# Merge turns by sevens in all four groups, a second seven in dilated pair 1, and two of four weight sums by accumulating DMAs

## The chip, the cores and the metric

The kernel runs on one core of a Trainium2 chip. Its time is the device time in microseconds (us) of one execution, the median of three runs. PE is the matmul engine (TensorE), DVE the vector engine (VectorE), ACT the scalar engine (ScalarE), POOL is GpSimd, SP is SyncE. The rows come from one profiled execution.

## The reference

One decoder layer on x of 256 tokens by 2048 columns, float32: a SwiGLU feed-forward (d_ff 5632), then two token mixers side by side (8 heads of dilated sliding-window attention with partial rotary, 8 heads of forgetting attention), merged by sigmoid gates, a second SwiGLU, a final RMSNorm.

```python
x = x + 0.5 * swiglu(rmsnorm(x, ffn1_norm), w_gate1, w_up1, w_down1)
proj = rmsnorm(x, mix_norm) @ w_in      # q_d k_d v_d q_f k_f v_f f_logit g_d g_f
merged = (sigmoid(g_d + b_gate_dil) * (y_dil @ w_proj_dil)
          + sigmoid(g_f + b_gate_fox) * (y_fox @ w_proj_fox))
x = x + merged @ w_out
x = x + 0.5 * swiglu(rmsnorm(x, ffn2_norm), w_gate2, w_up2, w_down2)
return rmsnorm(x, final_norm)
```

## The kernel before

Every float32 product is made of three matmuls in a reduced format: each operand is split into a rounded part (hi) and a rest (lo), and hi x hi, hi x lo and lo x hi are summed in PSUM. The weights come from HBM in loads of 1024 KB (`raw`, 4 buffers, `raw[:, l % LOADS]`), each holding 4 tiles of 128 rows by 512 columns. Two tiles are one *slab*. ACT rounds a slab into `w_hi`, DVE subtracts to get `w_lo`, PE multiplies. In the mixer part a ring of 4 slots (`MIX_RING`) holds the slabs: ACT rounds slab n + 4 when PE has done slab n (`slab_done`), DVE splits it when `hi_ready` says so, and PE waits for `lo_ready`. Each engine executes its own instructions in the order written.

Two weight matrices of the same width (called gate and up) times the two token tiles are four block products. Done directly, a group of 4 weight tiles of each is 4 slabs of 12 matmuls, 48 in all. *By seven* (Strassen-like), the group is 7 slabs of 6 matmuls, 42 in all, in exchange for sums. The token sums (`pair_sums`, `merge_pairs`, ...) are made once. The weight sums T3, T1, T2, T4 are made by DVE for every group (`dil_sum`, `merge_sum`), each over 128x1024 elements, into two buffers (T3 and T2 share one, T1 and T4 the other).

The parts in order: a first FFN (10 steps of 33 slabs), six *dilated pairs* (`dil_pair`; c = 0 to 5, of `D_SLABS` slabs, q/k, q/k, v for either mixer; with attention woven in), the first merge part (24 direct slabs of gate logits and projections, `MERGE_FIRST`), three *merge steps* (`merge(q)`, q = 0 to 2), a last down product and the second FFN. Of the pairs, c = 2 has two sevens and the others one.

A merge step of before has 41 slabs (`MERGE_STEP`): sevens at slabs 0, 9 and 18, the two direct gate slabs of group 3 at 7 and 8, its two direct up slabs at 16 and 17, 8 projection slabs from 25 (`M_PROJ_AT`), 8 down slabs from 33. DVE's order in it: at slab o it splits slab o + 4, with the sums of that slab's seven ahead of it; at o = 21 to 26 it combines the products into gate and up; after every second down slab it adds two banks into `xres` (`add_down`, L1872).

SP issues all weight loads in order, each behind a wait that the buffer's earlier slabs are split (`D_FREE`, `M_FREE`: the load l waits for that many slabs of the step). POOL issues in the FFNs the accumulating DMAs of the down products (`xres` += `gate_buf`, 512 KB, L1734), and nothing in the mixer part.

Of the kernel before, what the change touches and what calls it, by code (L numbers as in the profile page):

```python
# [19 lines left out]
F32 = mybir.dt.float32  # L20
# [45 lines left out]
D_SLABS, D_LOADS = (19, 19, 22, 19, 19, 19), 8  # L66
# [9 lines left out]
D_FREE = (_QK_FREE, _QK_FREE, _V_FREE, _QK_FREE, _QK_FREE, _QK_FREE)  # L76

D_SUMS, D_COMBINED = (0, 4, 8, 16, 20, 24), 5
# [4 lines left out]
M_PAIR_AT, M_PAIR_GROUPS, M_PAIR_LOADS = (0, 9, 18), (0, 1, 2), ((0, 1), (3, 4), (6, 7))  # L83
M_DIRECT_AT, M_DIRECT_GROUP, M_DIRECT_LOADS = (7, 16), 3, (2, 5)
# [3 lines left out]
M_PAIRS, M_SUMS, M_COMBINED = 3, 12, 5  # L88

M_THIRD, M_SPLIT_COUNT = 2, (1, 3, 2)  # L90
# [23 lines left out]
SUM_PLACE = {T3: 0, T2: 0, T1: 1, T4: 1}  # L114
SUMS_STEP = 4 * PAIRS
# [17 lines left out]
def merge_slab(r):  # L133

    for pair, first in enumerate(M_PAIR_AT):
        if first <= r < first + PAIR_SLABS:
            return "paired", pair, r - first
    for d, first in enumerate(M_DIRECT_AT):
        if first <= r < first + 2:
            return "direct", d, r - first  # L140
    return "rest", None, r - M_PROJ_AT
# [103 lines left out]
def build(nc, x, ffn1_norm, ffn1_w_gate, ffn1_w_up, ffn1_w_down, mix_norm, w_in, b_forget,  # L245
# [83 lines left out]
    tab_at = nc.sbuf_base  # L329
# [30 lines left out]
    gains = sb("gains", [P, 3 * KT])  # L360
    gain_rows = nc.alloc_sbuf_tensor_at("gain_rows", [KT, P], F32, offset=bias_at)
    squares = sb("squares", [P, TT, NN])
    end_sum = sb("end_sum", [P, TT])
    mean = sb("mean", [P, TT])
    root = sb("root", [P, TT])
    rstd = sb("rstd", [P, TT])
    rstd_q = sb("rstd_q", [P, TT])
    newton = sb("newton", [P, TT])
    neg_max = sb("neg_max", [P, TT])
    denom = sb("denom", [P, TT])  # L370
    inv_denom = sb("inv_denom", [P, TT])
# [4 lines left out]
    M1, M6, M7, M5, GATE, UP1, UP0 = 0, 1, 2, 3, 4, 6, 7  # L376
    DOWN_BANKS = (0, 2, 6, 4)
# [31 lines left out]
    def dil_sums_at(c, which):  # L409

        if c < F_PAIR:
            return dil_sums[:, SUM_PLACE[which]]
        return v_sb[:, SUM_PLACE[which], D_MIX:2 * D_MIX].rearrange("p (a b) -> p a b", b=CH)

    def dil_source(e):

        c, r, (kind, which, o) = dil_slab(e)
        if kind == "paired":
            what, part = PRODUCTS[o]
            if what == "sum":  # L420
                return dil_sums_at(c, part), None
            l = D_SEVEN[c][which][2][what == "gate"]
            return raw[:, l % LOADS, part::2, :], l
# [4 lines left out]
    def third_sums(x):  # L428


        return x[:, :, :].rearrange("p (g a b) c -> p g a b c", a=2, b=2)[:, 0:3, :, 0, P:2 * P]

    def merge_source(r):

        kind, which, o = merge_slab(r)
        if kind == "paired":
            what, part = PRODUCTS[o]
            if what == "sum":
                return merge_sums[SUM_PLACE[part]], None
            l = M_PAIR_LOADS[which][what == "gate"]  # L440
            return raw[:, l % LOADS, part::2, :], l
        l = M_DIRECT_LOADS[which] if kind == "direct" else M_PROJ_LOADS + o // 2
# [23 lines left out]
    dil_summed = sem("dil_summed")  # L466
    dil_m1_copied = sem("dil_m1_copied")
# [5 lines left out]
    merge_summed = sem("merge_summed")  # L473
    merge_m1_copied = sem("merge_m1_copied")
# [92 lines left out]
    DIL_TURNS = ((), (0, 1, 3, 4), (0, 1, 4, 6), (), (), ())  # L567
# [27 lines left out]
    with block:  # L595

        @block.sync
        def _(sp):
# [92 lines left out]
            for q in range(MERGES):  # L691
# [60 lines left out]
        def _(pe):  # L752
# [111 lines left out]
            def down(place, offset, count, base, next_too=False):  # L864
# [3 lines left out]
                for n in range(NN):  # L868
# [3 lines left out]
                    banks = down_banks(n)  # L872
# [155 lines left out]
            def dil_pair(c):  # L1028
# [26 lines left out]
                def seven_slab(s, group, o):  # L1055
                    bank, lhs = ((D_M7, of_sums(group, S3)), (D_M1, of_tile(group, 0, 0)),
                                 (D_M5, of_sums(group, S1)), (D_M6, of_sums(group, S2)),
                                 (D_UP0, of_sums(group, S4)), (D_GATES + 1, of_tile(group, 1, 1)),
                                 (D_GATES, of_tile(group, 1, 0)))[o]
# [178 lines left out]
            for g, banks in enumerate((A, C)):  # L1238
# [8 lines left out]
            def merge(q):  # L1247
# [3 lines left out]
                def of_pair(p, s):  # L1251
                    if p != M_THIRD:
                        return lambda j: (merge_hi[:, p, s, j], merge_lo[:, p, s, j])
                    if s == S4:
                        return lambda j: (fourth_hi[:, j], fourth_lo[:, j])
                    return lambda j: of_x(CT * s + 2 * j, 1)
# [1220 lines left out]
```

## Time and profile before

| | before |
|---|---|
| median of 3 runs | 2041.95 us (2041.85 to 2042.55) |
| span of the profiled execution | 2040.2 us |
| PE, DVE, ACT, POOL busy | 99%, 91%, 62%, 4% |
| weight loads (SP's queue) | 401.64 MB, 56.1% of 16 DMA engines |
| accumulating DMAs (POOL's queue) | 38.28 MB, 11.3% |

The profiled execution's own time is its span of 2040.2 us and what lies around it; the median of the runs is 1.75 us above the span. Busy times of matmuls overlap by pipelining, so the granted clock and the starts of matmuls say more than busy time.

### The profile page before, as it was taken

The numbers are of one execution on the slowest core, as the hardware profiler recorded it, in microseconds if no ns is written. First come the engines' busy times: TensorE is split into PE (matmuls) and PEld (weight loads), VectorE is DVE, ScalarE is ACT, GpSimd is POOL, SyncE is SP. The second block draws the span as 40 slices with busy tenths as digits, with TensorE's granted clock in tenths as the row PEclk, the third lists the DMA queues.
The fourth block names the chain that finished last, engine by engine and source line by source line (L and its number), as shares of the span: only waits on it lengthen the run. The fifth ranks groups of instructions, "written<-read, shape, count | busy, mean of one in ns | idle before, by whom it ended". The sixth has DMA issues, their size and how long they took to land.

```text
span 2040.2 us, 26364 instructions
## 1 busy us (share of the span) xinstructions
PE 2027.8 (99%) x9204; PEld 1678.7 (82%) x9204; DVE 1858.9 (91%) x1897; ACT 1267.5 (62%) x1474; POOL 87.6 (4%) x80
## 2 busy tenths in 40 slices
PE   9999999999999999999999999999999999999998
PEld 7888888888888888888888888888888888888886
DVE  7999999999999798887689999799999999999997
ACT  7666666666666556666556556466666666666664
POOL 0000000000000000000000000000000000000000
PEclk9999999999999999999999999999999999999999
DMA  8578777787877455554536575655878777877773
GB/s 301 206 211 259 230 236 246 227 236 227 246 247 235 157 186 183 198 177 157 183 134 227 189 243 182 211 186 192 242 223 250 244 232 211 260 225 240 247 231 127
DMA packets 222143, 441.03 MB, mean 216 GB/s; under 512 B 7648, under 2 KB 7824, under 8 KB 221936
## 3 DMA queue, kind: packets, MB, share of 16 engines
q1 hardware_dynamic: 202112, 401.64, 56.1%
q0 software_dynamic: 19744, 38.28, 11.3%
q8 instruction: 47, 0.77, 0.1%
q14 instruction: 32, 0.26, 0.0%
q10 hardware_dynamic: 208, 0.08, 0.0%
HBM read 400.13 MB, written 2.10 MB: 197 GB/s over the span
## 4 chain that ended last, share of the span: by engine, by line
PE 98%; DVE 1%; ACT 0%; DMA 0%; issue 0%; SPq 0%; ACTq 0%; DVEq 0%
PE ps L765 16%; PE ps L767 16%; PE ps L766 16%; PE ps L778 12%; PE ps L780 12%; PE ps L779 12%; PE ps L1002 2%; PE ps L1003 2%; PE ps L1001 2%; PE ps L1050 2%; PE ps L1052 2%; PE ps L1051 2%; PE ps L856 1%; PE ps L834 0%; DMA xres<-in_x 0%; PE ps L1169 0%
## 5 line engine op out<-in xcount | busy, mean ns | idle before, releaser
L1788 DVE TENSOR_TENSOR w_lo<-raw,w_hi 128x1024 fp32r<-128x1024 f32 x280 | 337.9, 1219 | 7.2 <-ACT w_hi L1356 4.9
L1356 ACT ACTIVATE w_hi<-raw 128x1024 fp32r<-128x1024 f32 x280 | 290.8, 1053 | 72.6 <-PE ps L767 54.0
L1356 ACT ACTIVATE w_hi<-sums 128x1024 fp32r<-128x1024 f32 x160 | 169.8, 1063 | 204.8 <-PE ps L767 71.4
L1788 DVE TENSOR_TENSOR w_lo<-sums,w_hi 128x1024 fp32r<-128x1024 f32 x160 | 195.3, 1222 | 33.8 <-ACT w_hi L1356 31.1
L765 PE MATMUL ps<-w_hi,hT_hi 128*128 128x512 f32 x536 | 208.8, 390 | 0.0
L767 PE MATMUL ps<-w_hi,hT_lo 128*128 128x512 f32 x536 | 208.5, 389 | 0.0
L766 PE MATMUL ps<-w_lo,hT_hi 128*128 128x512 f32 x536 | 208.5, 389 | 0.0
L1788 DVE TENSOR_TENSOR more_lo<-raw,more_hi 128x1024 fp32r<-128x1024 f32 x140 | 169.2, 1219 | 6.6 <-ACT more_hi L1356 5.6
L765 PE MATMUL ps<-w_hi,xT_hi 128*128 128x512 f32 x424 | 170.1, 401 | 0.0
L1356 ACT ACTIVATE more_hi<-raw 128x1024 fp32r<-128x1024 f32 x140 | 146.4, 1054 | 32.6 <-PE ps L767 23.8
L767 PE MATMUL ps<-w_hi,xT_lo 128*128 128x512 f32 x424 | 165.7, 391 | 0.0
L766 PE MATMUL ps<-w_lo,xT_hi 128*128 128x512 f32 x424 | 165.2, 390 | 0.0
L1734 POOL DMA_DIRECT2D xres<-gate_buf x72 | 84.9, 1179 | 1848.3 <-ACT gate_buf L1490 1803.3
L1356 ACT ACTIVATE more_hi<-sums 128x1024 fp32r<-128x1024 f32 x80 | 85.1, 1063 | 99.1 <-DVE sums L1770 24.1
L778 PE MATMUL ps<-w_hi,xT_hi 128*128 128x512 f32 x354 | 139.8, 395 | 0.0
L780 PE MATMUL ps<-w_hi,xT_lo 128*128 128x512 f32 x354 | 138.1, 390 | 0.0
L779 PE MATMUL ps<-w_lo,xT_hi 128*128 128x512 f32 x354 | 137.9, 390 | 0.0
L1675 ACT ACTIVATE w_hi<-raw 128x1024 fp32r<-128x1024 f32 x87 | 92.2, 1060 | 63.6 <-PE ps L767 51.8
L2128 DVE TENSOR_TENSOR w_lo<-raw,w_hi 128x1024 fp32r<-128x1024 f32 x85 | 102.2, 1220 | 20.2 <-ACT w_hi L1576 20.2
L1576 ACT ACTIVATE w_hi<-raw 128x1024 fp32r<-128x1024 f32 x85 | 89.1, 1057 | 47.2 <-PE ps L1052 31.0
L2317 DVE TENSOR_TENSOR w_lo<-raw,w_hi 128x1024 fp32r<-128x1024 f32 x87 | 104.8, 1220 | 14.9 <-ACT w_hi L1675 14.9
L767 PEld LDWEIGHTS ps<-w_hi,hT_lo 128*128 128x128 f32 x536 | 100.6, 188 | 20.9
(366 smaller groups left out, 5007.4 us busy)
## 6 DMA issues: line engine op xcount, KB each, us to landing
raw<-in_ffn_w_up SPq DMA_DIRECT2D x88, 1024.0 KB, 5.5
raw<-in_ffn_w_down SPq DMA_DIRECT2D x88, 1024.0 KB, 5.3
raw<-in_ffn_w_gate SPq DMA_DIRECT2D x87, 1024.0 KB, 5.4
raw<-in_w_in SPq DMA_DIRECT2D x80, 1024.0 KB, 5.0
xres<-gate_buf POOLq DMA_DIRECT2D x72, 512.0 KB, 5.5
raw<-in_w_out SPq DMA_DIRECT2D x16, 1024.0 KB, 5.1
raw<-in_w_proj_dil SPq DMA_DIRECT2D x8, 1024.0 KB, 5.5
raw<-in_w_proj_fox SPq DMA_DIRECT2D x8, 1024.0 KB, 5.2
```

Source lines behind the costliest of these rows:

```text
L765: nc.tensor.matmul(acc, hi, hi_w[:, j], start=first and j == 0, stop=False)
L766: nc.tensor.matmul(acc, hi, lo_w[:, j], start=False, stop=False)
L767: done = nc.tensor.matmul(acc, lo, hi_w[:, j], start=False, stop=last and j == 1)
L778: nc.tensor.matmul(acc, hi, hi_w[:, j], start=first and j == 0, stop=False)
L779: nc.tensor.matmul(acc, hi, lo_w[:, j], start=False, stop=False)
L780: done = nc.tensor.matmul(acc, lo, hi_w[:, j], start=False, stop=last and j == 1)
L1356: nc.scalar.activation(slot_hi(place, offset), src, ACT.Copy).then_inc(hi_ready, 1)
L1576: nc.scalar.activation(slot_hi(place, r), src, ACT.Copy).then_inc(hi_ready, 1)
L1675: nc.scalar.activation(slot_hi(place, offset), src, ACT.Copy).then_inc(hi_ready, 1)
L1788: nc.vector.tensor_tensor(slot_lo(place, offset), step_source(r)[0], slot_hi(place, offset).bitcast(F32), ALU.subtract).then_inc(lo_ready, 1)
L2128: nc.vector.tensor_tensor(slot_lo(place, r), dil_source(e)[0], slot_hi(place, r).bitcast(F32), ALU.subtract).then_inc(lo_ready, 1)
L2317: nc.vector.tensor_tensor(slot_lo(place, offset), merge_source(offset)[0], slot_hi(place, offset).bitcast(F32), ALU.subtract).then_inc(lo_ ...
```

## The change

In the merge steps all four groups are done by seven, at slabs 0, 7, 14 and 21; the direct slabs go. A step has 44 slabs. Dilated pair 1 takes the layout of pair 2, with a second seven (22 slabs). In all sevens of the mixer part the order of the products changes: gate 1, T3, T2, gate 0, up 1, T1, T4. DVE makes T3 and T2 only. T1 is made by a DMA from POOL that adds gate tiles into the up tiles of the raw buffer, T4 by one that adds T2 into the gate tiles. So T1 and T4 are read from the raw buffers, and these are freed by slabs 5 and 6 of the seven. Signs move into the token sums and into `rstd_n`. The combining adds of a merge step go from slabs 21 to 26 to slabs 25 to 28, with one add more (UP0 has its own bank), and the banks are numbered anew (`M_M1` ...; `merge_banks` swaps the down banks of all steps but the last). The token sums of the fourth group are made at slab 13 of the first merge part. Tables are laid out anew in SBUF. The FFNs are left as they are.

```diff
-D_SLABS, D_LOADS = (19, 19, 22, 19, 19, 19), 8
+D_SLABS, D_LOADS = (19, 22, 22, 19, 19, 19), 8
...
-D_SEVEN, D_GATE, D_UP = zip(_QK, _QK, _V, _QK, _QK, _QK)
-
-_QK_FREE, _V_FREE = (-6, -4, -2, 0, 2, 4, 6, 11), (-6, -4, -2, 0, 2, 7, 9, 11)
...
+D_SEVEN, D_GATE, D_UP = zip(_QK, _V, _V, _QK, _QK, _QK)
+
+_QK_FREE, _V_FREE = (-6, -4, -2, 0, 2, 4, 6, 12), (-6, -4, -2, 0, 2, 8, 9, 11)
...
-M_PROJ_AT, M_PROJ_LOADS, M_DOWN_AT, MERGE_STEP, MERGE_LOADS = 25, 8, 33, 41, 16
-
-M_FREE = (-6, -4, -2, 0, 5, 7, 9, 14, 16, 18, 23, 25, 27, 29, 31, 33)
...
+M_PAIR_AT, M_PAIR_GROUPS, M_PAIR_LOADS = (0, 7, 14, 21), (0, 1, 2, 3), ((0, 1), (2, 3), (4, 5), (6, 7))
+M_PROJ_AT, M_PROJ_LOADS, M_DOWN_AT, MERGE_STEP, MERGE_LOADS = 28, 8, 36, 44, 16
+
+M_FREE = (-6, -4, -2, 0, 6, 7, 13, 14, 20, 21, 27, 28, 30, 32, 34, 36)
...
+M_PRODUCTS = (("gate", 1), ("sum", T3), ("sum", T2), ("gate", 0), ("up", 1), ("sum", T1), ("sum", T4))
...
                 for o in seven(0):
-                    if o == 1:
+                    if q > 0 and o == 1:
+                        pe.wait_ge(gated, used + 2 * TT)
+                    if o == 2:
                         pe.wait_ge(gated, used + TT)
-                    if o == 5:
+                        pe.wait_ge(added, base)
+                    if q == 0 and o == 4:
                         pe.wait_ge(gated, used + 2 * TT)
-                        pe.wait_ge(added, base)
...
+                    part = M_PRODUCTS[o][1]
+                    if part == T1:
+                        act.wait_ge(merge_t1_added[pair], (q + 1) * 16)
+                    elif part == T4:
+                        act.wait_ge(merge_t4_added[pair], (q + 1) * 16)
...
+            def merge_add(q, p):
+
+                place, (up_l, gate_l) = merge_place(q), M_PAIR_LOADS[p]
+                up, gate = raw[:, up_l % LOADS], raw[:, gate_l % LOADS]
+                pool.wait_ge(merge_summed, q * M_SUMS + 2 * p + 1)
+                pool.wait_ge(raw_landed[gate_l % LOADS], place.landed(gate_l))
+                pool.dma_start(up[:, 0::2, :], gate[:, 0::2, :], accum_op=ALU.add)\
+                    .then_inc(merge_t1_added[p], 16)
+                pool.wait_ge(merge_summed, q * M_SUMS + 2 * p + 2)
+                pool.wait_ge(lo_ready, place.slab(M_PAIR_AT[p] + 1))
+                pool.dma_start(gate[:, 1::2, :], merge_sums[1], accum_op=ALU.add)\
+                    .then_inc(merge_t4_added[p], 16)
...
                 if which == T3:
-                    dve.wait_ge(lo_ready, place.slab(at - 2))
+                    if pair > 0:
+                        dve.wait_ge(lo_ready, place.slab(M_PAIR_AT[pair - 1] + 2))
                     dve.wait_ge(raw_landed[up_l % LOADS], place.landed(up_l))
-                    made = nc.vector.tensor_tensor(out, up[:, 1::2, :], up[:, 0::2, :], ALU.subtract)
...
+                    made = nc.vector.tensor_tensor(merge_sums[0], up[:, 1::2, :], up[:, 0::2, :], ALU.add)
+                else:
+                    if pair > 0:
+                        dve.wait_ge(merge_t4_added[pair - 1], (q + 1) * 16)
+                        dve.wait_ge(lo_ready, place.slab(M_PAIR_AT[pair - 1] + 3))
+                    elif q > 0:
+                        dve.wait_ge(merge_t4_added[M_PAIRS - 1], q * 16)
                     dve.wait_ge(raw_landed[gate_l % LOADS], place.landed(gate_l))
...
+                if kind == "paired" and o == 0:
+                    merge_sum(q, pair, T2)
+                if kind == "paired" and o == 5 and pair + 1 < M_PAIRS:
+                    merge_sum(q, pair + 1, T3)
+                if offset == MERGE_STEP - 2 and q + 1 < MERGES:
                     merge_sum(q + 1, 0, T3)
...
-                    if o == 21:
+                    if o == 25:
                         dve.wait_ge(merge_m1_copied, q + 1)
-                        dve.wait_ge(slab_done, place.slab(22))
-                        nc.vector.tensor_tensor(u2, ps[:, M6], partial[:, PART_M1],
+                        dve.wait_ge(slab_done, place.slab(25))
+                        nc.vector.tensor_tensor(u2, ps[:, M_M6], partial[:, PART_M1],
                                                 ALU.add).then_inc(merge_combined, 1)
```

The dilated pairs get the same: `dil_add` on POOL with the waits of `merge_add`, T2 ahead of the seven's first slab, T3 one slab before the seven.

## Rows read from the trace of the kernel before

**Rows 1.** The page: busy time, then slices of PE, its clock, and DMA.
```profile
PE 2027.8 (99%) x9204; PEld 1678.7 (82%) x9204; DVE 1858.9 (91%) x1897; ACT 1267.5 (62%) x1474; POOL 87.6 (4%) x80
...
PEclk9999999999999999999999999999999999999999
```

**Rows 2.** The page: the chain that ended last, by engine.
```profile
PE 98%; DVE 1%; ACT 0%; DMA 0%; issue 0%; SPq 0%; ACTq 0%; DVEq 0%
```

**Rows 3.** Windows over merge steps 0 and 1: window, busy us, clock, DMA share, GB/s.
```profile
1064.10:1149.50 85.40, 84.74 (x375) 69.28 (x374) 80.86 (x79) 46.55 (x48) 0.00 (x0) 1.00 0.61 205
1149.50:1233.60 84.10, 84.10 (x375) 69.40 (x375) 78.36 (x75) 46.86 (x48) 0.00 (x0) 1.00 0.62 207
```

**Rows 4.** Timeline of PE (start, us, what): slab 0 of steps 0, 1, 2; slab 1.
```profile
1064.13 0.39 PE L778 MATMUL ps<-w_hi,merge_hi 128*128 128x512 f32 x1
...
1149.54 0.39 PE L778 MATMUL ps<-w_hi,merge_hi 128*128 128x512 f32 x1
...
1150.90 0.39 PE L778 MATMUL ps<-w_hi,xT_hi 128*128 128x512 f32 x1
...
1233.62 0.39 PE L778 MATMUL ps<-w_hi,merge_hi 128*128 128x512 f32 x1
```

**Rows 5.** Timeline of ACT around the start of step 1.
```profile
1141.64 1.06 ACT L1675 ACTIVATE w_hi<-merge_sum 128x1024 fp32r<-128x1024 f32 x1 [1.66 <-PE ps L767]
1144.36 1.06 ACT L1675 ACTIVATE w_hi<-raw 128x1024 fp32r<-128x1024 f32 x1 [1.66 <-PE ps L767]
...
1149.80 1.06 ACT L1675 ACTIVATE w_hi<-merge_sum 128x1024 fp32r<-128x1024 f32 x1 [1.66 <-PE ps L767]
1151.16 1.06 ACT L1675 ACTIVATE w_hi<-raw 128x1024 fp32r<-128x1024 f32 x1 [0.30 <-PE ps L780]
```

**Rows 6.** Timeline of DVE around the start of step 1.
```profile
1142.73 1.23 DVE L2317 TENSOR_TENSOR w_lo<-merge_sum,w_hi 128x1024 fp32r<-128x1024 f32 x1 [0.36 <-ACT w_hi L1675]
...
1151.26 1.22 DVE L2317 TENSOR_TENSOR w_lo<-merge_sum,w_hi 128x1024 fp32r<-128x1024 f32 x1
1152.39 1.22 DVE L1872 SCALAR_TENSOR_TENSOR xres<-ps,xres 128x1024 f32<-128x1024 f32 x1
1153.53 1.22 DVE L2317 TENSOR_TENSOR w_lo<-raw,w_hi 128x1024 fp32r<-128x1024 f32 x1
```

**Rows 7.** Instructions of line 1734, the accumulating DMAs: ns min/median/max, then landing.
```profile
L1734 POOL DMA_DIRECT2D xres<-gate_buf x72: 1168/1179/1222, 104.4 to 1949.6; - x72
...
DMA to landing us min/median/max: 5.2/5.5/9.0
```

**Rows 8.** The four of one FFN step, issued at 228.62, 234.15, 239.50, 244.93: landing.
```profile
DMA to landing us min/median/max: 8.9/8.9/8.9
...
DMA to landing us min/median/max: 7.3/7.3/7.3
...
DMA to landing us min/median/max: 5.3/5.3/5.3
...
DMA to landing us min/median/max: 5.6/5.6/5.6
```

**Rows 9.** Windows: us, POOL busy, clock, DMA share, GB/s; accumulate alone, then loads.
```profile
241.00:244.00 3.00, 0.00 (x0) 1.00 1.05 171
...
1138.00:1140.00 2.00, 0.00 (x0) 1.00 1.02 396
1158.00:1161.00 3.00, 0.00 (x0) 1.00 1.04 403
```

**Rows 10.** Groups of DVE from 1040 to 1059, ahead of step 0: token sums.
```profile
L2326 DVE TENSOR_TENSOR merge_x<-xT_hi,xT_lo 128x1024 f32<-128x1024 f32 x1 | 1.2, 1217 | 0.0
L2346 DVE TENSOR_TENSOR merge_lo<-merge_pairs,merge_hi 128x1024 fp32r<-128x1024 f32 x1 | 1.2, 1216 | 0.0
...
L2330 DVE TENSOR_TENSOR merge_third<-merge_x 128x256 f32<-128x256 f32 x1 | 0.4, 424 | 0.0
```

**Rows 11.** SP's loads from 1136 to 1190: issue to landing.
```profile
DMA to landing us min/median/max: 4.8/5.0/5.8
```

More of the change, by code:

```diff
@@ L418, in dil_source @@
         if kind == "paired":
-            what, part = PRODUCTS[o]
+            what, part = D_PRODUCTS[o]
+            up_l, gate_l = D_SEVEN[c][which][2]
+            if what == "sum" and part in (T3, T2):
+                return dil_sums_at(c, part), None
             if what == "sum":
-                return dil_sums_at(c, part), None
-            l = D_SEVEN[c][which][2][what == "gate"]
+                return raw[:, (up_l if part == T1 else gate_l) % LOADS, (part == T4)::2, :], None
+            l = gate_l if what == "gate" else up_l
             return raw[:, l % LOADS, part::2, :], l
@@ L436, in merge_source @@
         if kind == "paired":
-            what, part = PRODUCTS[o]
+            what, part = M_PRODUCTS[o]
+            up_l, gate_l = M_PAIR_LOADS[which]
+            if what == "sum" and part in (T3, T2):
+                return merge_sums[part == T2], None
             if what == "sum":
-                return merge_sums[SUM_PLACE[part]], None
-            l = M_PAIR_LOADS[which][what == "gate"]
+                return raw[:, (up_l if part == T1 else gate_l) % LOADS, (part == T4)::2, :], None
+            l = gate_l if what == "gate" else up_l
             return raw[:, l % LOADS, part::2, :], l
-        l = M_DIRECT_LOADS[which] if kind == "direct" else M_PROJ_LOADS + o // 2
+        l = M_PROJ_LOADS + o // 2
         return raw[:, l % LOADS, o % 2 * 2:o % 2 * 2 + 2, :], l
@@ L1237, in _ @@
                     e += 1
-            for g, banks in enumerate((A, C)):
+            for g, banks in enumerate((A, T)):
                 pe.wait_ge(gate_pre, (g + 1) * TT)
@@ L1570, in round_dil @@
                 src, l = dil_source(e)
-                if l is None:
-                    act.wait_ge(dil_summed, D_SUMS[c] + 4 * which + PRODUCTS[o][1] + 1)
+                part, seven = D_PRODUCTS[o][1] if kind == "paired" else None, D_BEFORE[c] + which
+                if l is None and part in (T1, T4):
+                    added_by = dil_t1_added if part == T1 else dil_t4_added
+                    act.wait_ge(added_by[seven % 2], (seven // 2 + 1) * 16)
+                elif l is None:
+                    act.wait_ge(dil_summed, 2 * seven + (part == T2) + 1)
                 else:
@@ L2200, in _ @@
                 if r == last + 6:
+                    dve.wait_ge(slab_done, place.slab(last + 6))
                     dve.wait_ge(dil_combined, merged + 2)
```

312 lines of the change are left out of this document (152 added, 160 removed).

## The prediction

> **What bounds the kernel now.** I read the page first. PE is busy for 99% of the span at a granted clock of full speed, and DVE for 91% [rows 1]. The chain that ended last is PE for 98% [rows 2]. So a PE instruction less is a gain, and every wait that PE gets is a loss: there is no slack in which to hide one. Next I read the stretch that the change rebuilds. One merge step of before takes 84.1 us with PE busy for 84.10 of 84.10 us, DVE for 78.4 us; the first of the three takes 85.4 us with PE busy for 84.74 [rows 3]. The starts of slab 0 say the same: 1064.13, 1149.54 and 1233.62, so 85.41 and 84.08 us [rows 4]. The first step therefore holds 1.3 us of stall and the second none.
>
> Then the pace of the engines inside the step. Two slabs of one product begin at 1149.54 and 1150.90: 1.36 us for 6 matmuls [rows 4]. ScalarE, which rounds slab n + 4 when slab n is done, starts every 2.72 us in the direct part and every 1.36 us in the turns by seven [rows 5]. A VectorE operation over 128x1024 takes 1.22 us, but the next starts 1.13 to 1.14 us after it (1151.26, 1152.39, 1153.53) [rows 6]; I use 1.135. So a seven costs PE 7 x 1.36 = 9.5 us, and VectorE in before 7 splits and 4 sums, 11 x 1.135 = 12.5 us. VectorE is the slower one in every seven. What saves before is the pair of direct slabs between the sevens: 9 slabs are 15.0 us of PE and 13 x 1.135 = 14.8 us of VectorE.
>
> **The change, part by part.** (1) *Matmuls.* A group done directly is 48 matmuls, by seven 42. One group per merge step and one in dilated pair 1 change: 4 x 6 x 0.227 = 5.4 us less on PE, of it 1.36 us per merge step.
>
> (2) *VectorE.* Per seven, T1 and T4 go to accumulating DMAs, so 7 splits and 2 sums stay: 9 x 1.135 = 10.2 us, still above PE's 9.5 us. But the four sevens of a merge step now follow each other over 28 slabs, 38.1 us of PE, with no direct slab between. The lead that PE has is small: the weight ring has 4 slots, and a split is through 0.26 us (ScalarE's start) + 1.09 (rounding) + 1.22 = 2.6 us after its slot came free, while PE needs it 3 x 1.36 = 4.1 us after. That is 1.5 us of slack.
>
> (3) *The accumulating DMAs.* T4 is the one to follow. POOL issues it after T2 is summed and slab 0 of the seven is split, because it adds into the bytes that slab 0 reads. Queued behind it: ScalarE waits for it before it rounds slab 6 of the same seven, and its in-order queue holds slab 7 behind that. VectorE waits before the split of slab 6, and behind that stands T2 of the next seven, which overwrites the operand that the DMA reads. Then comes slab 0 of the next seven, which releases the next T4. It is a closed loop. With L from issue to landing, one turn of it is 0.1 (semaphore, estimated) + L + 1.09 (rounding, 1141.64 to 1142.73) + 1.135 (split of slab 6) + 1.135 (T2) + 1.22 (split of slab 0) = L + 4.7 us [rows 5, 6]. It costs nothing only if L is below 9.5 - 4.7 = 4.8 us. The same kind of DMA, 512 KB in SBUF accumulated by POOL, took 5.2 us at least, 5.5 in the median and 9.0 at most, of which 1.18 us is POOL's issue [rows 7]. So no L in the trace fits.
>
> Which L? The four of one FFN step landed after 8.9, 7.3, 5.3 and 5.6 us [rows 8]. The short ones had the DMA engines to themselves at first, the long ones had loads beside them. Alone, an accumulate moves 171 GB/s with the engines full (241 to 244); loads move 396 to 403 GB/s [rows 9]. A seven of the new merge step needs two loads of 1.05 MB, 2 x 2.6 us, and two accumulates of 0.52 MB, 2 x 3.1 us: 11.4 us of full engines per seven of 9.5 us of PE. The weight loads are freed by splits 5 and 6 of a seven (the new list of free slots), so they start 2 to 3 us before T4 every time. L is then a contended one. I take 7.3, the row with a load in flight for part of the time; 5.3 and 8.9 are the ends.
>
> (4) *The sum of a merge step*, zero at PE's start of slab 0. Split 3 starts at 0.26 + 1.09 = 1.35. Then follow the residual add, split 4, T3, splits 5 and 6, T2 and split 7, seven pitches on: split 7 starts at 9.3 and is done at 10.5. T4 of the second seven: split 13 starts at 10.5 + 0.1 + L + 1.09 = 11.7 + L. Split 14 is done at 15.2 + L, split 21 one loop later at 19.9 + 2L, split 27 at 22.3 + 3L, and PE ends slab 27 at 23.7 + 3L. Without waits it would be 38.1, so the loss is 3L - 14.4. T4 of the first seven is covered by four direct slabs. One more wait comes behind it: slab 28 writes the banks of M1 and M6, and the add that reads them (now at slab 25, before at 21 with the projections at 25) stands behind splits 28 and 29: 3.4 us after split 27 starts plus 0.7, against PE's 1.22 + 1.36, so 1.5 us. The wait for the residual add, moved from product 5 to product 2 of the first seven, costs 3.7 - 2.7 = 1.0 us there, but the wait at slab 13 swallows it (PE would ask at 18.7, the split is done at 20.2). Per step: 3L - 14.4 + 1.5 - 1.36 = 3L - 14.3, which is +7.6 us at 7.3. At L = 5.3 VectorE's own 10.2 us per seven is the slower: split 21 done at 10.5 + 2 x 10.2 = 30.9, split 27 at 30.9 + 0.1 + 5.3 + 1.09 + 1.22 = 38.6, PE's end 40.0, so +2.0. At 8.9 it is +12.4.
>
> (5) *The first merge step* held 1.3 us of stall already, which these waits replace: -1.3. Its fourth group of token sums adds a 1.22 us add, four of 0.42 us and a split of 1.22 us on VectorE, and one copy on ScalarE [rows 10]. They lie beside direct slabs of 2.72 us with 1.135 us of split each; nothing, and up to 1.3 us if that cover is gone, since VectorE has no gap there from 1049.8 on.
>
> (6) *Dilated pairs.* Pair 1 gains 1.36 us. In the other five only sums move, where PE already waits for nothing, so VectorE's relief is worth 0. T4 there has direct slabs beside it. The tightest is the second seven of pairs 1 and 2, whose gate load is freed one split later (8 for 7). Counted from the end of slab 3, that load is issued at about 2.6 and landed at about 8 (loads landed 4.8 to 5.8 us after issue [rows 11]), split 11 is done at 10.4, T4 landed at 17.8, split 17 done at 20.1. PE asks at 5 x 1.36 + 2 x 2.72 + 6 x 1.36 = 20.4. So 0; at L = 8.9 it is 1.3 us in each, 2.6 together. POOL's queue holds nothing else in this part.
>
> Sum: 3 x 7.6 - 1.3 - 1.4 = **+20.1 us**. The profiled execution has a span of 2040.2 us, 1.75 us below the median of 2041.95 us; that remainder is launch and end, and stays. Forecast: 2041.95 + 20.1 = **2062 us**.
>
> **A rule of the Trainium skill.** An accumulate with full engines moved 171 GB/s here [rows 9]. The Trainium skill, page "DMA: Bandwidth & Descriptors", section "Where 436 GB/s comes from", says that for transfers from SBUF to SBUF the fabric side of 435 GB/s binds. By it, as an estimate, an accumulate would need 1.2 us, and the change would come out as in rival A. The trace speaks against it, with its 171 GB/s.
>
> **The rivals.** *A: no loss, VectorE alone sets the pace.* If L is 3.6 us or less (5.3 less the 1.7 us or so by which a transfer at the loads' 400 GB/s is shorter), the loop is 8.3 us and the sevens run at 10.2. Then split 27 is done at 30.9 + 6 x 1.135 = 37.7, PE ends at 39.1, and a step is 1.0 + 1.5 - 1.36 = +1.1: in all 3.3 - 2.7 = +0.6, so 2042.6 us. With L = 5.3 it is 3 x 2.0 - 2.7 = +3.3, 2045 us. For it: the short landings. Against it: each T4 has loads before it. Together 0.10. *B: faster.* If the loop does not bind and the add at slab 25 is in time, PE's 5.4 us and the 1.3 us of the first step come back: 2035 us. It decides at L + 4.7 below 9.5 and needs VectorE below 9.5 us per seven too, and nine pitches are 10.2. 0.03. *C: full engines.* The 11.4 us of DMA per seven put T4 behind both loads each time: L = 8.9, 3 x 12.4 - 2.7 + 2.6 = +37, 2079 us. For it: the engines are asked for more than they give. Against it: as the loop lengthens, the demand falls to 11.4 of 12 us. 0.17. *The forecast*, L from about 6 to 8.3: 0.70.
>
> **How the numbers follow.** The range goes from the short landing (2045) to C (2079). Changes under about 0.2%, 4 us, can't be told from none. Slower is the forecast with C, 0.87; within 0.2% is A, 0.10; faster is B, 0.03.
>
> **What would show it.** In the changed kernel's profile: PE idle of some 20 us or more, nearly all inside the three merge steps, released by splits of slabs 13, 14, 20, 21 and 27 and by the add before slab 28; POOL's accumulates with a landing near 7 us; slab 0 of the steps some 92 us apart; the FFNs unchanged. ScalarE's waits there would name the accumulating DMA. If the landing is below 5.5 us in the merge steps, or the steps are under 86 us, the loop argument is wrong. If the loss lies in the dilated pairs, step 6 is.

## The result and the profile after

The changed kernel takes 2086.43 us (median of 5 runs, 2083.32 to 2087.92), the kernel before 2042.08 us beside it: a ratio of 1.0214, with a 95% interval of 1.0202 to 1.0226. The forecast was 2062 us with a range of 2045 to 2079. The sign was right, the loss more than twice the forecast, and above the range. The profiled execution took 2084.43 us with a span of 2082.6 us.

The page of the changed kernel: busy time, granted clock, the chain that ended last by engine and by line (to set beside [rows 1] and [rows 2]).

```profile
PE 2038.6 (98%) x9180; PEld 1679.2 (81%) x9180; DVE 1848.7 (89%) x1893; ACT 1279.1 (61%) x1486; POOL 134.8 (6%) x120
...
PEclk9999999999999999999999999999999999999999
...
PE 88%; DMA 5%; DVE 4%; ACT 1%; issue 1%; SPq 0%; ACTq 0%; DVEq 0%; POOLq 0%
PE ps L781 15%; PE ps L783 15%; PE ps L782 15%; PE ps L794 10%; PE ps L796 10%; PE ps L795 10%; DMA raw<-merge_sum 4%; PE ps L1019 2%; PE ps L1017 2%; PE ps L1018 2%; DVE w_lo L2357 1%; PE ps L1066 1%; PE ps L1068 1%; PE ps L1067 1%; PE ps 
```

PE has 24 matmuls less and is busy for 10.8 us more, which no count of instructions explains. T4's DMA (raw<-merge_sum), which was not there, stands on the chain for 4% of the span. The windows over the three merge steps, from slab 0 to slab 0 and the last to the first slab after it (columns as in [rows 3]):

```profile
1068.76:1163.87 95.11, 86.86 (x369) 68.81 (x368) 79.96 (x78) 48.86 (x51) 9.84 (x9) 0.98 0.88 242
1163.87:1261.95 98.08, 88.21 (x369) 70.19 (x368) 76.61 (x73) 49.30 (x51) 9.42 (x8) 0.95 0.77 220
1261.95:1361.23 99.28, 89.85 (x378) 72.07 (x376) 75.79 (x73) 50.29 (x53) 7.07 (x6) 0.93 0.70 206
```

In the kernel before they took 85.41, 84.08 and 85.03 us. The last, from 1233.62 to 1318.65, has PE busy throughout:

```profile
1233.60:1318.60 85.00, 85.00 (x383) 70.26 (x382) 76.80 (x74) 47.82 (x50) 0.00 (x0) 1.00 0.60 203
```

So the steps cost +9.7, +14.0 and +14.3 us, and slab 0 of the first starts 4.6 us later (1068.76 for 1064.13 [rows 4]): +42.6 us in all, the whole difference of the spans (42.4). The FFNs and everything behind are unchanged. Two things stand in the columns: PE's idle time (8 to 10 us per step), and a granted clock of 0.95 and 0.93 where it was 1.00, with PE busy for 88 to 90 us on work that took 84.

The chain through step 1 (start, us, what), without its short pieces of idle time:

```profile
1170.90 1.22 DVE w_lo L2357
1172.12 1.14 DVE merge_sum L2338
1173.26 1.15 DVE w_lo L2357
...
1174.93 9.65 DMA raw<-merge_sum
1184.61 1.06 ACT w_hi L1679
...
1186.84 1.22 DVE merge_sum L2338
1188.06 1.15 DVE w_lo L2357
...
1189.79 6.40 DMA raw<-merge_sum
1196.21 1.07 ACT w_hi L1679
...
1198.45 1.22 DVE merge_sum L2338
1199.67 1.14 DVE w_lo L2357
...
1201.55 9.78 DMA raw<-merge_sum
1211.36 1.06 ACT w_hi L1679
...
1212.45 1.24 DVE w_lo L2357
```

This is the closed loop of the prediction's step 3, operation by operation: T4's DMA, the rounding of slab 6, its split (at 1185.70 and 1197.3, which the chain shows as a gap), T2 (L2338), the split of slab 0, the next DMA. From 1174.93 to 1189.79 it takes 14.86 us with a landing of 9.65, from there to 1201.55 11.76 with 6.40, so L + 5.2 and L + 5.4; I had L + 4.7. The rest is POOL's start, 0.6 us after the split of slab 0 is done (1188.06 + 1.15), which I had estimated at 0.1. The landings of T4's DMA over the three steps, and a row each of a matmul behind the last wait of step 1 and of the same kind of matmul later:

```profile
L1754 POOL DMA_DIRECT2D raw<-merge_sum x12: 1179/1179/1200, 1068.0 to 1299.7; - x12
...
DMA to landing us min/median/max: 5.0/7.4/9.8
```

```profile
1213.73 0.80 PE L794 MATMUL ps<-w_hi,xT_hi 128*128 128x512 f32 x1 [4.19 <-DVE w_lo L2357]
1214.32 0.63 PE L795 MATMUL ps<-w_lo,xT_hi 128*128 128x512 f32 x1
1214.75 0.63 PE L796 MATMUL ps<-w_hi,xT_lo 128*128 128x512 f32 x1
...
1222.29 0.39 PE L781 MATMUL ps<-w_hi,yT_hi 128*128 128x512 f32 x1
1222.51 0.39 PE L782 MATMUL ps<-w_lo,yT_hi 128*128 128x512 f32 x1
```

The matmuls after the idle 4.19 us start 0.43 us apart instead of 0.23. The windows say the same (the granted clock is the third figure from the end):

```profile
1213.70:1217.90 4.20, 4.17 (x9) 2.94 (x10) 4.17 (x5) 3.10 (x4) 0.00 (x0) 0.50 0.70 239
1220.00:1224.00 4.00, 4.00 (x19) 3.31 (x18) 3.96 (x6) 1.84 (x2) 0.00 (x0) 1.00 0.83 278
```

So PE was granted half its clock, 1.2 GHz for 2.4, after it had been idle for 4.19 us. It happens again after idle times of 3.97, 4.16 and 3.71 us (at 1186.97, 1285.24 and 1311.58), and in step 0 after 1.99 us:

```profile
1091.83 0.68 PE L794 MATMUL ps<-w_hi,xT_hi 128*128 128x512 f32 x1 [1.99 <-DVE w_lo L2357]
```

The stretches at half clock last 3.5 to 5.7 us. The Trainium skill, page "TensorE: Matmul & The Clock Gate", section "Loop structure matters more than you think", warns of it: a loop in which matmuls wait for DMAs runs them at the lower clock. The trace agrees, and the prediction had no such term.

### The profile page after: what moved, and what is told of

Its sections match the earlier page's. It is cut to its first block, busy times and chain, and to the rows that moved or that the text cites. A ratio compares the mean times of both kernels' runs of the same rounds, so it can differ in the third digit from the quotient of the medians.

```text
span 2082.6 us, 26407 instructions
## 1 busy us (share of the span) xinstructions
PE 2038.6 (98%) x9180; PEld 1679.2 (81%) x9180; DVE 1848.7 (89%) x1893; ACT 1279.1 (61%) x1486; POOL 134.8 (6%) x120
## 4 chain that ended last, share of the span: by engine, by line
PE 88%; DMA 5%; DVE 4%; ACT 1%; issue 1%; SPq 0%; ACTq 0%; DVEq 0%; POOLq 0%
PE ps L781 15%; PE ps L783 15%; PE ps L782 15%; PE ps L794 10%; PE ps L796 10%; PE ps L795 10%; DMA raw<-merge_sum 4%; PE ps L1019 2%; PE ps L1017 2%; PE ps L1018 2%; DVE w_lo L2357 1%; PE ps L1066 1%; PE ps L1068 1%; PE ps L1067 1%; PE ps L872 1%
## 5 line engine op out<-in xcount | busy, mean ns | idle before, releaser
L1832 DVE TENSOR_TENSOR w_lo<-raw,w_hi 128x1024 fp32r<-128x1024 f32 x280 | 337.9, 1219 | 6.9 <-ACT w_hi L1350 4.6
L1350 ACT ACTIVATE w_hi<-raw 128x1024 fp32r<-128x1024 f32 x280 | 290.8, 1053 | 72.4 <-PE ps L783 53.7
L1679 ACT ACTIVATE w_hi<-raw 128x1024 fp32r<-128x1024 f32 x108 | 112.9, 1057 | 131.1 <-PE ps L783 64.8
L794 PE MATMUL ps<-w_hi,xT_hi 128*128 128x512 f32 x384 | 156.8, 408 | 24.8 <-DVE w_lo L2357 23.7
L2357 DVE TENSOR_TENSOR w_lo<-raw,w_hi 128x1024 fp32r<-128x1024 f32 x108 | 130.2, 1220 | 55.3 <-ACT w_hi L1679 55.3
L2170 DVE TENSOR_TENSOR w_lo<-raw,w_hi 128x1024 fp32r<-128x1024 f32 x100 | 121.2, 1222 | 41.2 <-ACT w_hi L1574 38.3
L781 PE MATMUL ps<-w_hi,xT_hi 128*128 128x512 f32 x392 | 157.4, 401 | 0.0
L1574 ACT ACTIVATE w_hi<-raw 128x1024 fp32r<-128x1024 f32 x100 | 104.9, 1057 | 63.5 <-PE ps L1068 25.4
```

Source lines behind the costliest of these rows:

```text
L781: nc.tensor.matmul(acc, hi, hi_w[:, j], start=first and j == 0, stop=False)
L794: nc.tensor.matmul(acc, hi, hi_w[:, j], start=first and j == 0, stop=False)
L1350: nc.scalar.activation(slot_hi(place, offset), src, ACT.Copy).then_inc(hi_ready, 1)
L1574: nc.scalar.activation(slot_hi(place, r), src, ACT.Copy).then_inc(hi_ready, 1)
L1679: nc.scalar.activation(slot_hi(place, offset), src, ACT.Copy).then_inc(hi_ready, 1)
L1832: nc.vector.tensor_tensor(slot_lo(place, offset), step_source(r)[0], slot_hi(place, offset).bitcast(F32), ALU.subtract).then_inc(lo_ready, 1)
```

## The experiments

All runs are set against the kernel before on the same chip (2041.9 to 2042.2 us). The table gives what most of them are read by: where slab 0 of the first merge step starts, the length of the three steps (slab 0 to slab 0), the mean granted clock over the span, and T4's landing in them (minimum, median, maximum). The kernels below the second row differ from it only from the merge steps and their loads on, and yet their slab 0 starts anywhere from 1068.8 to 1072.2: differences in time of 2 to 3 us between single kernels say little, the lengths of the steps say more.

| kernel | us | ratio, 95% interval | slab 0 | steps | clock | T4 landing |
|---|---|---|---|---|---|---|
| before | 2042.1 | | 1064.1 | 85.4, 84.1, 85.0 | 0.999 | |
| after | 2086.4 | 1.0202 to 1.0226 | 1068.8 | 95.1, 98.1, 99.3 | 0.992 | 5.0/7.4/9.8 |
| T1 and T4 by VectorE | 2075.0 | 1.0141 to 1.0175 | 1070.6 | 96.2, 92.1, 93.1 | 0.998 | |
| T1 by VectorE | 2070.9 | 1.0121 to 1.0155 | 1069.7 | 92.8, 92.5, 92.4 | 0.999 | 5.0/6.4/8.2 |
| T4 by VectorE | 2075.0 | 1.0140 to 1.0174 | 1071.4 | 94.4, 91.7, 95.4 | 0.997 | |
| half of T4's bytes | 2073.9 | 1.0138 to 1.0172 | 1070.1 | 92.1, 94.1, 93.2 | 0.998 | 3.3/7.2/8.1 |
| light loads, sevens | 2073.2 | 1.0137 to 1.0171 | 1071.2 | 93.2, 92.6, 93.0 | 0.993 | 5.0/5.0/9.9 |
| light loads, all | 2056.6 | 1.0057 to 1.0087 | 1071.7 | 87.2, 86.8, 87.6 | 0.998 | 5.0/5.0/5.5 |
| loads held back | 2101.7 | 1.0272 to 1.0306 | 1072.2 | 105.4, 101.2, 102.4 | 0.988 | 5.0/5.0/9.1 |
| PE kept busy | 2083.2 | 1.0186 to 1.0220 | 1069.7 | 95.8, 94.9, 99.1 | 0.997 | 5.0/7.1/10.3 |

**Both sums by VectorE.** Without POOL's queue, in place:

```diff
-                pool.dma_start(up[:, 0::2, :], gate[:, 0::2, :], accum_op=ALU.add)\
...
-                pool.dma_start(gate[:, 1::2, :], merge_sums[1], accum_op=ALU.add)\
...
+                    nc.vector.tensor_tensor(raw[:, up_l % LOADS, 0::2, :], raw[:, up_l % LOADS, 0::2, :],
+                                            raw[:, gate_l % LOADS, 0::2, :], ALU.add)\
...
+                    nc.vector.tensor_tensor(raw[:, gate_l % LOADS, 1::2, :], raw[:, gate_l % LOADS, 1::2, :],
+                                            merge_sums[1], ALU.add).then_inc(merge_t4_added[pair], 16)
```

> In the merge steps both T1 and T4 are added by VectorE in place, into the same bytes, instead of by POOL's DMAs; the layout of four sevens stays, the dilated pairs keep their DMAs. Theory (loop through the accumulating DMA): the loop is gone, VectorE's own work sets the pace: 37 pitches of 1.135 us from split 3 to split 27, so PE ends slab 27 at 45.9 us instead of 38.1, a step is about +8 us on before, no wait of PE over 2 us, and the clock stays at full speed: 2071 us. Rival 1 (the accumulates are the whole loss): 2045 to 2050 us. Rival 2 (VectorE was the bound all along in the changed kernel): adding two operations per seven makes it worse than the changed kernel, over 2090 us.

2075.0 us for 2071 expected. T3 (L2321) of two sevens one after the other in the chain of step 1:

```profile
1184.08 1.22 DVE merge_sum L2321
...
1196.57 1.22 DVE merge_sum L2321
```

12.49 us: the 11 operations of 1.135 us of the prediction, against PE's 9.5. Four sevens without direct slabs between them lose some 8 us in steps 1 and 2 (10.8 in step 0) with no DMA at all, because VectorE is slower than PE in each. The accumulating DMAs were meant to take that away, and cost more than it.

**One of the two by VectorE.**

> In the merge steps T1 is added by VectorE in place, T4 stays with the DMA. Loop theory: T4's landing gets shorter because one accumulate per seven less competes (from 8 to 9 us down to 6 to 7), the loop is then near VectorE's ten operations, 11.35 us per seven: +5 to +8 us per step, 2061 to 2072 us. Rival (T4's landing does not depend on the other accumulate): VectorE's extra operation fits in its waits and nothing changes, 2084 to 2088 us.

Inside the range, 2070.9 us. T4's landing fell from 7.4 to 6.4 us in the median although T4 itself is untouched: T1's 512 KB were part of its contention. The loop with 6.4 + 5.2 = 11.6 us and VectorE's 10 operations (11.35 us) are then nearly level.

> In the merge steps T4 is added by VectorE in place, T1 stays with the DMA. Loop theory: T1 is not in the loop, so VectorE's ten operations set the pace: 34 pitches to split 27, PE's slab 27 ends at 42.5, +4.5 us per step, no half clock: 2061 us. Rival (any accumulate in these stretches costs its landing): close to the changed kernel, over 2075 us.

A miss: 2075.0 us for 2061, and at the edge of what the rival said. I had looked at T4's loop alone. Its chain in step 1 shows another one behind it:

```profile
1185.42 10.25 DMA raw<-in_w_in
...
1196.32 10.26 DMA raw<-raw
...
1207.69 2.88 DVE w_lo L2359 x3
```

The gate load of the fourth seven takes 10.25 us where loads took 5.0 in the median [rows 11], T1's DMA may only start when it has landed and takes 10.26, and only then is the slab of T1 rounded. Load and accumulate follow each other, both slow.

**Fewer bytes.** Half of T4's operand is left out:

```diff
-                pool.dma_start(gate[:, 1::2, :], merge_sums[1], accum_op=ALU.add)\
+                pool.dma_start(gate[:, 1:2, :], merge_sums[1][:, 0:1], accum_op=ALU.add)\
```

> The DMA that makes T4 in the merge steps moves only one of its two tiles, 256 KB, so half of T4 is left without its sum; instructions and waits are the same. Loop theory: landing shorter by 1.5 to 2 us, each step by about 3 times that, 4.5 to 6 us, and fewer half-clock stretches: 2066 to 2072 us. Rival (VectorE's pace or the weight loads are the bound): within 3 us of the changed kernel.

2073.9 us, just above its range: half of T4's bytes give back 12.5 us of the 44. The shortest landing fell from 5.0 to 3.3 us and the longest from 9.8 to 8.1, the median only from 7.4 to 7.2. On the chain of step 1 the three are 8.1, 7.2 and 7.4 us for 9.65, 6.4 and 9.8. So T4's own bytes are a part of its landing and of what the DMA engines are asked for, but with half of them it still lands 4 us later than the 3.3 of the shortest. Next, the loads:

```diff
-                    load_merge(l, in_w[:, CT * g:CT * (g + 1), col:col + CH])
+                    sp.wait_ge(lo_ready, place.slab(M_FREE[l]))
+                    sp.dma_start(raw[:, l % LOADS, 0:1], in_w[:, CT * g:CT * g + 1, col:col + CH])\
+                      .then_inc(raw_landed[l % LOADS], 16)
```

> The changed kernel, but each of the eight weight loads of the sevens in a merge step brings only a quarter of its bytes (256 KB for 1 MB), so that part of the computation works on stale weights; every wait, sum and accumulating DMA is as it was. My theory: the accumulating DMAs land late because loads share the DMA engines with them. Then the landing of T4's falls from 7.4 in the median to 5.0 to 5.8 us, VectorE's own 10.2 us per seven becomes the pace, a merge step costs about +2 us on before instead of +10 to +14, and the time is about 2042 + 5 (up to the first step) + 6 = 2053 us, 2050 to 2060. Rival: the accumulate is slow by itself (reads and writes of one memory at 171 GB/s, descriptors written by POOL); then the landing stays at 7 us and more and the time above 2068 us.

Neither: the landing fell to 5.0 us in the median, as the theory has it, and the time only to 2073.2 us. The chain shows where the theory stopped short. T2 (L2340), the split that follows and T4's DMA of the last two sevens of step 1:

```profile
1182.84 1.22 DVE merge_sum L2340
...
1193.06 1.22 DVE merge_sum L2340
1194.28 1.15 DVE w_lo L2359
...
1196.17 9.87 DMA raw<-merge_sum
```

The sevens now follow at 10.2 us, VectorE's nine operations, but the last T4 takes 9.87 us: the projection loads, which were left whole, are freed right before it. One late DMA per step, and the half clock behind it, keeps most of the loss. The next run cuts the projection loads as well.

> As the run with light loads in the sevens, but the four projection loads of each merge step are cut to a quarter too (they are freed from the split of slab 20 on, and in that run the last T4 of a step landed after 9.9 us beside them, the others after 5.0). My theory: any full load beside an accumulating DMA makes it late; without them T4 lands after 5.0 to 5.8 us all four times, no PE wait above 1.6 us is left, the granted clock is 1.00, and each merge step gives back 4.9 us of landing and 1 to 1.5 us of half clock: 2073.2 - 3 x 6 = 2055 us, 2052 to 2060. Rival: the last T4 of a step is late for another reason (the adds, POOL's queue); then 2070 us and more.

2056.6 us, inside the range. The windows line of step 1, for 98.08 us and a clock of 0.95 in the changed kernel:

```profile
1158.90:1245.73 86.83, 83.93 (x370) 68.00 (x368) 76.41 (x73) 49.13 (x51) 9.43 (x8) 1.00 0.58 140
```

A step costs +2.8 us on before, where the prediction's low end (L = 5.3) said +2.0. The three steps together are 7 us longer than before, for 38 us in the changed kernel: what the loads do beside the accumulates is 31 of the 38. The other 7.6 of this run's 14.5 us lie ahead of slab 0. T4's landing is 5.0 us without full loads and 6 to 10 beside them. What the run doesn't separate is T4 from the rest, since with fewer bytes the loads and T1's DMA land sooner too (T1 after 6.3 us in the median for 7.1).

**Could the order save it?** The same bytes, with loads that wait until T4 has landed:

```diff
+M_HELD_BY = {4: 1, 5: 1, 6: 2, 7: 2, 9: 3}
...
                     sp.wait_ge(lo_ready, place.slab(M_FREE[l]))
+                    if l in M_HELD_BY:
+                        sp.wait_ge(merge_t4_added[M_HELD_BY[l]], (q + 1) * 16)
```

> The changed kernel, computing all that it should, with five of the sixteen loads of each merge step held back: the loads of the third and fourth seven until T4 of the seven before has landed, and the second projection load until T4 of the fourth has. SP's queue holds nothing but loads, so the wait delays these and the ones behind them. No accumulating DMA for T4 then meets a load that was freed just before it. My theory: T4 lands after 5 to 6 us for 7.4 in the median, the waits above 3 us are gone, and the time falls to 2058 to 2070 us, though all bytes are still moved. Rival: with 11.4 us of DMA per seven of 10 to 12 us a load that starts 5 us later comes too late itself, and ScalarE waits for loads instead of T4: 2080 us and more.

The rival: 2101.7 us. T4 lands after 5.0 us in the median, as wanted. Its chain:

```profile
1188.67 5.18 DMA raw<-merge_sum
1193.91 5.19 DMA raw<-in_w_in
1199.19 1.23 DVE merge_sum L2332
```

What had run beside each other now runs one after the other, and T3 waits for the load. So the late landing was a symptom of full DMA engines. While the T4 issued at 1174.93 was under way in the changed kernel, with T1's DMA and three loads, the engines were full at 262 GB/s:

```profile
1171.00:1185.00 14.00, 12.00 (x53) 9.47 (x51) 10.21 (x9) 6.55 (x7) 1.51 (x2) 1.00 0.99 262
```

A seven wants 3.1 MB moved, and at 262 GB/s that is 12.0 us for 9.5 us of PE (worked out, not measured by itself). The prediction's 11.4 us, from 400 GB/s for loads and 171 for accumulates, is 276 GB/s for the same bytes and so was nearly right.

**The half clock.** Twelve matmuls of 512 columns into a bank that nobody reads, ahead of slabs 13, 20 and 27:

```diff
+                        if o == 6 and p > 0:
+                            for n in range(12):
+                                nc.tensor.matmul(ps[:, 3, :], xT_hi[:, 0, 0:P], xT_hi[:, 0:2, :],
+                                                 start=n == 0, stop=n == 11)
```

> The changed kernel with 12 more matmuls of 512 columns, into a bank that nothing reads, ahead of slabs 13, 20 and 27 of each merge step, where PE waits up to 4.2 us for the split; nothing that is computed changes. They fill 2.7 us of each wait, so that PE isn't idle long. My theory: part of the loss is the half clock that PE is granted after the long waits (matmuls every 0.43 us for 0.23, in five places); then the mean granted clock is 1.00 for 0.992 and the time 2078 to 2083 us for 2086.4. Rival: the half clock lies beside the next wait of the same loop and costs nothing, or no more than the added matmuls do where a wait is shorter than 2.7 us; then the time is 2085 to 2089 us.

2083.2 us (2082.7 to 2084.7) for 2086.4 (2083.3 to 2087.9), clock 0.997 for 0.992: just above the theory's range and below the rival's. The intervals of the two ratios overlap, so the time doesn't settle it. The traces do in part: step 1 fell from 98.1 to 94.9 us, step 2 stayed (99.1), and step 0 went from 95.1 to 95.8, since there the added matmuls are longer than some waits.

**Ahead of the first step.** The two parts that I had costed at nothing, each taken out. The fourth group's token sums first (the operations of the slot with index 13 left out, a copy of 8 columns in their place):

> The changed kernel without the token sums of the fourth group (five VectorE operations in the last slots of the attention part), so that the fourth seven of each merge step works on other sums than it should. My theory: they are what delays the start of the first merge step, beyond the 2.9 us that pair 1 costs; the time falls by 1.5 to 3 us, to about 2084 us. Rival: the first step's first accumulating DMAs wait for loads and splits anyway, so that what is won ahead of it is given back in it: 2086 us, within 0.5.

2085.0 us, with an interval (1.0189 to 1.0223) that overlaps that of the changed kernel: unclear by the time. The traces tell it: in the changed kernel the heads' part has one wait, which this run doesn't have (PE 14.00 of 14.00 us).

```profile
1054.20 0.67 PE L1185 MATMUL ps<-probsT,v_sb 128*128 128x256 f32 x2 [0.98 <-DVE yT_lo L2194]
```

```profile
1043.00:1057.00 14.00, 14.00 (x72) 11.75 (x71) 10.14 (x20) 8.85 (x16) 0.00 (x0) 1.00 0.11 23
```

Then T1 and T4 of the dilated pairs by VectorE in place:

> The changed kernel with T1 and T4 of the dilated pairs summed by VectorE in place (two operations of 128x1024 more per seven there) instead of by accumulating DMAs; the merge steps are as they were. My theory: pair 1 loses 1.5 + 1.4 us because T4 lands 9.1 us after its issue and the copies of the pair's end come behind that; with VectorE the second seven of pair 1 has no late DMA, and the time falls by 1.5 to 3 us, to about 2084 us. Rival: VectorE at 12.5 us per seven is just as late in the second seven as the DMA was, or later in the other pairs too: 2086 to 2092 us.

2086.9 us: no gain, and my theory for pair 1 fell. The two waits for splits of the second seven (0.35 and 0.89 us, step 6 below) are gone in this run. The third wait isn't, and in the profiled execution PE has half its clock for 3.5 us behind it. The first transposes of pair 1's values, in the changed kernel and in this one:

```profile
799.97 0.63 PE L1031 MATMUL ps<-tab,gate_buf 128*128 128x128 f32 x4 [2.20 <-issue]
```

```profile
799.30 0.63 PE L1031 MATMUL ps<-tab,gate_buf 128*128 128x128 f32 x4 [2.78 <-issue]
```

The wait is there without a DMA. What they wait for is the rotation on VectorE (the changed kernel, then the end of the rotation and the transposes in the kernel before):

```profile
797.32 1.22 DVE L2170 TENSOR_TENSOR w_lo<-dil_sums,w_hi 128x1024 fp32r<-128x1024 f32 x1
...
799.59 0.28 DVE L2133 TENSOR_TENSOR gate_buf<-rope_a,rope_b 128x128 f32<-128x128 f32 x1
```

```profile
792.34 0.29 DVE L2088 TENSOR_TENSOR gate_buf<-rope_a,rope_b 128x128 f32<-128x128 f32 x1
...
796.87 0.60 PE L1015 MATMUL ps<-tab,gate_buf 128*128 128x128 f32 x4
```

The rotation is tied to ten slabs after the start of the last seven. With one seven at slab 6 it ran at 791.2 to 792.6, and the transposes at 796.87 had 4.2 us to spare; with the last seven at slab 11 it ends at 799.9, while the transposes stay behind slab 0 of the next pair. To test that, the kernel before with this part of the change alone, all sums by VectorE:

```diff
-D_SLABS, D_LOADS = (19, 19, 22, 19, 19, 19), 8
+D_SLABS, D_LOADS = (19, 22, 22, 19, 19, 19), 8
...
-    DIL_TURNS = ((), (0, 1, 3, 4), (0, 1, 4, 6), (), (), ())
+    DIL_TURNS = ((), (0, 1, 4, 6), (0, 1, 4, 6), (), (), ())
```

> The kernel before with one part of the change alone: the second seven in dilated pair 1, all four of its sums by VectorE, merge steps untouched. PE does 6 matmuls less, 1.36 us. In the changed kernel the transposes of pair 1's values waited 2.2 us, because with a second seven the last combining adds and the rotation come 2.7 us and more later while the transposes stay after slab 0 of pair 2. My theory: the same wait is here, and the time is 2042.1 - 1.4 + 2.2 = 2042.9 us, 2042 to 2044. Rival: the 2.2 us came from the accumulating DMAs; then it is 2040.7 us.

2044.5 us, a ratio of 1.001 (1.0001 to 1.0019) in 11 runs: 6 matmuls less make it slower by 2.3 us, somewhat above the range. Its row and the window behind it:

```profile
798.82 1.09 PE L1015 MATMUL ps<-tab,gate_buf 128*128 128x128 f32 x4 [2.25 <-issue]
```

```profile
798.80:802.00 3.20, 3.18 (x10) 2.72 (x11) 2.19 (x2) 0.75 (x2) 0.00 (x0) 0.51 0.02 5
```

The wait is there, and behind it PE has half its clock for some 3 us, 1.5 us more, which the expectation hadn't. The same idle time doesn't always bring it: in the changed kernel's profiled execution the clock behind the 2.20 us is 1.00, and the 11 runs here fall into five of 2043.3 to 2043.8 us, with a mean clock of 0.999, and six of 2044.5 to 2045.4, with 0.998. Without the stretch the theory's range holds. The version with the first two transposes a slab later, pair 2's list being (1, 2, 4, 6):

> As the run before it, with the first two transposes of pair 1's values one slab of pair 2 later each (after slabs 1 and 2 for 0 and 1). A slab is 2.7 us there, so the wait of 2.2 us should be gone and nothing new should wait: theory 2040.7 us, 2040.2 to 2041.5, the one version that is faster than both. Rival: VectorE is too busy with two sevens in pair 1 (12.5 us per seven against 9.5 of PE) and PE waits for splits instead: 2042 us and more.

```profile
801.80 0.63 PE L1015 MATMUL ps<-tab,gate_buf 128*128 128x128 f32 x4 [0.45 <-ACT qT L1559]
```

The wait of 2.25 us is gone; the second transpose now follows the first by a slab and waits 0.45 us for ScalarE's copy. 2041.7 us, just above the theory's range, ratio 0.9999 (0.9990 to 1.0008): all 11 runs are below all 11 of the version with the wait, but of the 1.36 us saved too little is left to be measured against the kernel before. No version beat the kernel before.

## Why the prediction fell short

**What held.** What bounds the kernel, the pace of the engines (VectorE 10.2 us per seven, measured 10.2; 12.49 with 11 operations), and the closed loop: its members, its place and its releaser are those of the chain. POOL's 1.18 us of issue, too. The ends of L were about right: 5.0 alone, 9.8 beside loads, for 5.3 and 8.9 taken. Of the 22.5 us that were missing (42.6 for 20.1) 16.5 lie in the merge steps (38.0 for 21.5) and 6 ahead of them (+4.6 for -1.4).

**Step 3, the size of L.** I took 7.3. The three of the formula landed after 7.7, 7.1 and 7.1 us in step 0, but 9.65, 6.4 and 9.8 in step 1 and 9.8, 6.5 and 9.5 in step 2 (the 6.5 level with PE's own way). Put into the step's own formula, sum of L - 14.3: step 1 is 25.8 - 14.3 = +11.5 and step 2 25.8 - 14.3 = +11.5, for +7.6 each. That is 8 us of the 22.5 us that were missing. The sign of the mistake was in the prediction: it had the demand, 11.4 us of full engines per seven, from 400 and 171 GB/s, found it below the lengthened loop in rival C, and let it count against C. The demand was nearly right (12.0 us at the 262 GB/s measured), but full engines make every landing late, T1's and the gate load's too. "As the loop lengthens, the demand falls" was the sentence that failed: the mean fits, while the loads come in bursts right ahead of T4 (argued from the window above; no run moved them ahead).

**Step 4, the start of T4 and the clock.** Measured less formula is 14.0 - 11.5 = 2.5 us in step 1 and 14.3 - 11.5 = 2.8 in step 2. Slab 27 starts 49.9 and 49.6 us after slab 0 (1213.73 and 1311.58) where the formula with the measured landings has 48.1: POOL starts T4 0.5 to 0.7 us behind the split, for 0.1 estimated, three times a step, together 1.5 to 1.8 us. The rest is the half clock behind the last wait, for which the step had no term. It lasts 4.5 us in step 1 and 5.7 in step 2, but costs less than half of that, since its first 2.87 us, slab 27, PE would have spent anyway: the add before slab 28 holds it up (1.36 + 1.5 in the sum), and in step 0 and in the run with T1 by VectorE slab 28 starts 2.87 and 2.88 us after slab 27 at full clock. What comes after costs: from slab 28 to the first transposes behind it PE takes 9.09 and 9.61 us for 8.31 at full clock in step 0, so 0.8 and 1.3 us. Behind the middle waits of a step the half clock lies beside the next wait of the loop. The split of the bill is read from the traces; the run that kept PE busy got back 3 us, but its interval overlaps.

**Steps 4 and 5, the first step and its approach.** The fourth group's sums were put at 0, up to 1.3; they are 1.1 us (the last stretch between two head products takes 7.60 us, 1046.60 to 1054.20, for 6.47 before and in the run without the sums). The step itself was put at +6.3 and was +9.7, with L as forecast. "T4 of the first seven is covered by four direct slabs" failed there. POOL's rows for it in step 0 and in step 1:

```profile
1067.97 1.18 POOL L1754 DMA_DIRECT2D raw<-merge_sum  x1 [2.04 <-DVE w_lo L2357]
...
1159.51 1.18 POOL L1754 DMA_DIRECT2D raw<-merge_sum  x1 [5.20 <-DVE w_lo L2357]
```

In step 1 it starts 4.4 us before slab 0 and split 7 is done at 10.5 us, as the step has it. In step 0 it starts only 0.8 us before slab 0, lands after 8.65 us and stands at the head of the chain, and split 7 is done at 12.5: 2.0 of the 3.4 us missing. POOL's later starts, as above, fit the rest. VectorE works without a gap ahead of it, and the gate load that T2 reads has landed only at 1064.1; which of the two makes it late was not tried by itself. The fourth group's sums alone don't: without them T4 still starts only 1.3 us before slab 0.

**Step 6, dilated pair 1.** Forecast -1.4, measured +3.1 (the first transposes 799.97 for 796.87): 0.35 and 0.89 us for splits of the second seven and 2.20 us for the rotation, which with the 1.36 us saved make +2.1; the last 1.0 us is assigned to no row. The step asked only whether slabs were split in time. It did not follow what is tied to the seven's end, the combining adds, the evacuation and the rotation, while what needs them stayed where it was. In pair 2, T4 costs 0 to 1.8 us from run to run.

**The rivals.** C, with a chance of 0.17, had the mechanism and nearly the size, 2079 us. But its L of 8.9 each time wasn't measured either (7.3, 8.6 and 8.6 in the mean of a step), and the later starts of T4 and the clock, which it lacked, made up for it: its 36 us for the steps against 38.0 owe something to luck. The rule on the fabric's rate, by which an accumulate would be short enough for rival A (the Trainium skill, "DMA: Bandwidth & Descriptors", "Where 436 GB/s comes from"), finds no support: with all loads of the sevens and projections cut to a quarter T4 still lands after 5.0 us, where A needs 3.6 or less, and the time is 2056.6 us for A's 2042.6.

## What to carry to other kernels

A DMA that replaces an engine's work is priced by its landing beside the loads that the same edit frees, not by its median elsewhere, and when the mixed demand fills the DMA engines, holding loads back only moves the wait (the one order tried here cost 15 us more). When a stage is made longer or its last part later, list what is tied to its end and what stands at a fixed place behind it. Where PE will wait for as long as here (2 to 4 us), look for a stretch at half clock behind the wait and bill half of it, but only as far as nothing else would have waited there (here 0.8, 1.3 and 1.5 us of stretches of 4.5, 5.7 and 3 us).

## What was not expected of the hardware

An accumulating DMA of 512 KB within SBUF landed after 5.0 us at best and 9.8 us at most in the merge steps of the changed kernel; one of 256 KB after 3.3 us at best, 7.2 in the median and 8.1 at most. Beside it a load of 1 MB took 10.25 us for 5.0. The engines were full (share 0.99) at 262 GB/s. PE's clock fell to 0.50 after idle times of 3.7 to 4.2 us, once after 1.99 and once after 2.25 us, and the matmuls then ran 0.43 us apart for 3 to 5.7 us. After 2.20 us of idle time ahead of the same transposes it stayed at 1.00 in one execution (the changed kernel's) and fell to 0.50 in another (that of the run with all loads light).
